# Two layers of a hybrid decoder trunk on one core: groups of two picks, adds ahead of some rows, and a reordered opening

## The reference

```
h = rms_norm(x);  proj = h @ w_in          # q, k, v, forget logits, pool part, state-space part
x = x + concat(norm(attention), norm(pool), norm(s5)) @ w_out
h = rms_norm(x)                            # PEER
q = h @ w_q;  scores against 2 x 128 sub-keys per head (8 heads)
top 16 of each half -> 256 candidates -> top 16 -> expert index = i1*128 + i2, gates = softmax
u_sel, v_sel = u_tab[experts], v_tab[experts]       # 128 picks per token, rows of 1024 floats
x = x + sum_k gate_k * gelu(h . u_sel_k) * v_sel_k
```

## Time and profile before

| what | value |
|---|---|
| median of three runs | 1546.36 us |
| profiled execution, its own time | 1547.98 us |
| its span from first to last instruction | 1546.1 us |
| granted TensorE clock, mean over the span | 0.826 |
| busy in the span | DVE 70%, PE 68%, POOL 40%, ACT 37% |
| moved in the span | 623.55 MB, 403 GB/s on average |
| q0 (gathers) | 536.90 MB, 83.7% of the 16 engines' span |
| q1 (SP's transfers) | 85.41 MB, 13.4% |

### The profile page before, as it was taken

How to read it: one execution, slowest core, us unless ns; L and a number is a source line. 1 busy time by engine, 2 the same in 40 slices (tenths; PEclk the granted TensorE clock), 3 DMA queues, 4 the chain that set the end, 5 groups by cost and what they waited for, 6 DMA issues and landing times. The chain is left out here.

```text
span 1546.1 us, 19439 instructions
## 1 busy us (share of the span) xinstructions
PE 1049.1 (68%) x6790; PEld 532.8 (34%) x6790; DVE 1083.2 (70%) x2485; ACT 575.1 (37%) x1768; POOL 619.7 (40%) x571
## 2 busy tenths in 40 slices
PE   8898656785854668776775667788588465565555
PEld 6685312333531334332552334333255111111111
DVE  8777998646999685654789767564579965444444
ACT  5544433623444433441544431354234432221222
POOL 0034345442753533443343433444243354455441
PEclk9999877887986988787897788889698777667767
DMA  9289999999999999999999999999999999999997
GB/s 381 89 326 421 420 421 420 421 421 405 422 421 368 411 422 421 421 421 421 409 421 421 421 421 421 421 422 420 422 386 421 421 421 422 421 421 422 421 421 304
DMA packets 86642, 623.55 MB, mean 403 GB/s; under 512 B 10000, under 2 KB 10128, under 8 KB 11792
## 3 DMA queue, kind: packets, MB, share of 16 engines
q0 software_dynamic: 73728, 536.90, 83.7%
q1 hardware_dynamic: 12816, 85.41, 13.4%
HBM read 621.23 MB, written 1.05 MB: 402 GB/s over the span
## 5 line engine op out<-in xcount | busy, mean ns | idle before, releaser
L583 POOL DMA_INDIRECT slots<-experts,idx x512 | 593.2, 1159 | 886.5 <-PE psum L1830 709.9
L1427 DVE CUSTOM_DVE_ANT_0 slots<-slots,h 128x1024 f32<-128x1024 f32 x512 | 615.9, 1225 | 390.8 <-DMA slots<-experts,idx 387.6
L1830 PE MATMUL psum<-slots,diag 64*64 64x512 f32 x4088 | 599.3, 737 | 312.4 <-ACT diag L947 312.3
L1830 PEld LDWEIGHTS psum<-slots,diag 64*64 64x64 f32 x4088 | 175.8, 165 | 684.2 <-ACT diag L947 368.9
L931 ACT ACTIVATE ge<-ge 128x4 f32<-128x4 f32 x130 | 26.7, 205 | 437.3 <-DVE ge L1427 436.3
L1752 PE MATMUL psum<-hT,ring 128*128 128x128 f32 x992 | 131.3, 297 | 20.7 <-DMA ring<-weights 16.0
L931 ACT ACT_TABLE_LOAD x55 | 70.6, 1283 | 194.7 <-DVE ge L1427 194.3
L947 ACT ACTIVATE diag<-cst,ge 128x64 f32<-128x64 f32 x511 | 136.5, 336 | 6.7 <-PE psum L1830 2.5
L1752 PEld LDWEIGHTS psum<-hT,ring 128*128 128x128 f32 x992 | 127.7, 212 | 23.5 <-issue 17.7
L938 ACT ACTIVATE ge<-ge,gate 128x1 f32<-128x1 f32 x512 | 109.1, 283 | 4.2
L1525 PE MATMUL psum<-ring,hT 128*128 128x256 f32 x192 | 52.2, 433 | 17.5 <-DVE work L981 17.5
(11 more groups left out here) (292 smaller groups left out, 1075.4 us busy)
## 6 DMA issues: line engine op xcount, KB each, us to landing
ring<-weights SPq DMA_DIRECT2D x32, 1152.0 KB, 10.0
ring<-weights SPq DMA_DIRECT2D x26, 1024.0 KB, 9.2
slots<-weights SPq DMA_DIRECT2D x11, 1024.0 KB, 20.0
slots<-experts,idx POOLq DMA_INDIRECT x512, 20.8
ring<-weights SPq DMA_DIRECT2D x2, 1056.0 KB
sml<-small SPq DMA_DIRECT2D x2, 652.0 KB, 9.1
slots<-weights SPq DMA_DIRECT2D x1, 1056.0 KB, 9.0
xs<-x SPq DMA_DIRECT2D x2, 512.0 KB, 13.2
```

Source lines behind the costliest of these rows:

```text
L583: pool.indirect_dma_start(out=slot[:, place(E), :], out_offset=None, in_=src, in_offset=bass.IndirectOffsetOnAxis(ap=idx[:, n % 2, e:e + 1 ...
L1427: ins = dve.tensor_tensor_reduce(u, u, h2[:, n % 2, :], 1.0, 0.0, ALU.mult, ALU.add, d[:, i:i + 1])
L1830: ins = pe.matmul(acc[HALF * half:HALF * half + HALF, i, :], diag[rows, d % DIAGS, :], slot[rows, place(E), D + half * 512:D + half * 512 ...
```

## The change

There are four edits.

1. `GRP` is 2 in place of 4: 64 groups a step. A group is weighed and added by itself, and a row now stands at the next border of two picks. The last two picks remain groups of one.
2. A new piece `adds` on PE: ahead of a row that contains one of the twelve names in `FOLLOWS`, PE adds the group that is waiting, which otherwise it would do behind the row.
3. `MIX0` is in another order. `mul1` and `mul2` come behind `cm`, `mul3` behind `mixp`. `qkn0` (the sums of squares) comes ahead of `scan0`, and the subtraction of `scan0` becomes a piece of its own (`scan_im`) behind `qkn1`. At the end of `MIX0`, `p`, `qkv0` and `qkv1` of step 1 come ahead of the routing of head 1.
4. SP loads the first q block right behind the chunk of the pool part.

```
-GRP = 4
+GRP = 2
...
-        "power4", "qkv0", "f", "prep", "fx", "ln", "mul0", "mul1", "mul2", "mul3", "rotate0", "rotate1", "cum", "cm",
-        "qkv1", "rotate2", "bu", "qkv2", "scan0", "qkv3", "qkn0", "scan1", "qkn1", "qkv4", "pool", "qkT", "pre0", "pre1",
-        "mixp", "sq1", "scan2", "scan3", "scan4", "scan5", "scan6", "logits0", "scan7", "big0", "logits1", "scan8",
...
+        "power4", "qkv0", "f", "prep", "fx", "ln", "mul0", "rotate0", "rotate1", "cum", "cm", "mul1", "mul2",
+        "qkv1", "rotate2", "bu", "qkv2", "qkv3", "qkn0", "scan0", "qkn1", "scan_im", "qkv4", "pool", "qkT", "pre0", "pre1",
+        "mixp", "mul3", "sq1", "scan1", "scan2", "scan3", "scan4", "scan5", "scan6", "logits0", "scan7", "big0", "logits1",
...
+        "route0", ("xT", 1), ("hTe", 1), "rp1", ("u", 1), "soft0", ("uT", 1), ("p", 1), ("up", 1), ("qkv0", 1),
+        ("f", 1), ("fx", 1), ("ln", 1), ("qkv1", 1), "route1", "soft1", ("cum", 1), ("cm", 1), ("qkv2", 1), ("qkv3", 1),
...
+FOLLOWS = {"normT", "u", "qkv0", "y", "glu", "qkT", "att1", "att2", "att3", "att4", "out0", "h2T"}
...
                 step, row = rows[at]
+                if FOLLOWS.intersection(row):
+                    order.append(("mix", "adds", n))
                 order += [("mix", s, 2 if s[:3] == "tab" else step) for s in row]
...
             chunk(CH_SSM)
             chunk(CH_POOL)
+            chunk(CH_Q)
             sp.dma_start(cst[:, P:], consts[:, P:]).then_inc(S["cst_in"], 16)
             drive_(0)
             rest_(0)
-            for i in range(6):
+            for i in range(1, 6):
                 chunk(CH_Q + i)
...
+            def scan_im(n):
+                link(tt(w3[1], w3[1], w3[3], ALU.subtract))
...
                 if part % 9 == 0:
                     link(tt(w3[0], w3[0], spare, ALU.add))
-                    link(tt(w3[1], w3[1], w3[3], ALU.subtract))
+                if part == 9:
+                    scan_im(n)
...
+            def adds(n):
+                add_last()
```

More of the change, by code:

```diff
@@ L136, in script @@
                 order += [("mix", "soft" + s[5:], step) for s in row if s[:5] == "route"]
-    for quad in (QUADS, QUADS + 1):
-        order += [("open", n, quad), ("close", n, quad)]
-    return order + [("mix", "drain", STEPS - 1)]
+    return order + [("open", n, QUADS), ("close", n, QUADS), ("mix", "drain", STEPS - 1)]
 ORDER = script()
@@ L191, in experts_of @@
     start, end = PICKS * n + GRP * quad, PICKS * n + GRP * quad + GRP
[L192 to L195, removed]
+    last = PICKS * STEPS - 1
+    return range(start, min(end, last)) if start <= last else range(last, last + 1)
 BY_VECTOR = {PICKS * STEPS - 1}
@@ L203, in by_tensor @@
     return sum(1 for e in range(E) if e not in BY_VECTOR)
-G_LAST = QUADS * STEPS + 1
+G_LAST = QUADS * STEPS
 SECTION = (slice(0, 512), slice(512, 768), slice(768, 1024))
@@ L1428, in dots @@
                 told(ins, "dots_ready")
-            run(dict(inverse=inverse, fold=fold, attg=attg, x1p=x1p, x1a=x1a, h2=h2_, power=power, rotate=rotate_, normA=normA, normT=normT, uT=u_out, cum=cum,
+            run(dict(scan_im=scan_im, inverse=inverse, fold=fold, attg=attg, x1p=x1p, x1a=x1a, h2=h2_, power=power, rotate=rotate_, normA=normA, normT=normT, uT=u_out, cum=cum,
                      warm=blank, h2T=h2T, turnback=turnback, bu=bu, scan=scan, backA=back, backB=back_im, y=y_, glu=glu, qkn=qkn, qkT=qkT,
@@ L1838, in close @@
                 waiting.append((n, quad))
-            run(dict(warm=warm, pre=pre, logits=logits0, turn=turn0, pv=pv0, normT=normT, xT=normT, u=u, p=p_, f=f_, oua=out_a, bu=bu, qkv=qkv, y=y_, glu=glu, qkT=qkT, att=att, pool=pool_,
+            run(dict(adds=adds, warm=warm, pre=pre, logits=logits0, turn=turn0, pv=pv0, normT=normT, xT=normT, u=u, p=p_, f=f_, oua=out_a, bu=bu, qkv=qkv, y=y_, glu=glu, qkT=qkT, att=att, pool=pool_,
                      mixp=mixp, merge=merge, out=out_b, h2T=h2T, rp=rp, route=route), lambda n, quad: None, close)
```

## The result

The changed kernel takes 1551.45 us (median of 8 runs, 1548.9 to 1552.9) against 1546.5 (8 runs): ratio 1.0028, 95% interval 1.0019 to 1.0037. It is 4.3 us slower by the ratio, where 9.4 us faster was forecast. The profiled execution took 1550.07 us, its span is 1548.3.

What follows compares the result with a forecast made beforehand. Transfers at 421 GB/s bound most of the span, DVE's routing the 450 us stretch; 1.9 + 5.8 + 1.7 = 9.4 us off 1547.98 gives 1538.6, as a median 1537.0. Range 1534.5 to 1540; over all cases 1532.5 to 1544.5.

Steps and rivals of the forecast that it cites:

- The opening: Start up to the first gather: first maximum and all after it 1.9 us earlier.
- the four times shown above: Opening: sum of squares at 35.27 us, scaling from about 38.1, first maximum 46.1, first gather near 84.3.
- 0.2 us in hand for the squares: Opening: ACT's squares ready near 35.1 us, just in time for DVE's sum at 35.27.
- The row h2T: Near 370, 750 and 1120 us: slots freed earlier keep transfers full, 5.8 us won over three steps.
- length x (1 - rate/421): The prediction's measure of time in which transfers stand, per window; the short ones add up to 11.5 us.
- The end of step 0: 450 to 515 us: DVE waits 0.8 us per routing row; transfers stand 4.0 instead of 5.7 us, 1.7 won.
- It holds: Up to about 250 us: six routing rows cost 4.8 us, covered by 4.2 in hand and pairs freed 3.2 earlier.
- the end of step 2: Said to have six such routing rows too; a hole near 1240 us would make the forecast wrong.
- PE's adds cost nothing where transfers are full: Other stretches: PE's adds, like the doubled number of gelus, were priced at nothing.
- The slower rival: Routing rows where DVE is the bound: wait spreads, 2.1 us a row, 1552.7 us; decides from 1.2; chance 0.07.
- the wait behind the pair: Routing rows: DVE waits for ACT's score copy behind a pair's weighing, 0.8 us taken, 2.1 in the slower rival.

Runs made afterwards that it cites:

- e2: The kernel before with only the adds ahead of the twelve kinds of rows, in groups of four with the old opening: ratio 1.0005.
- e5: The kernel before, in groups of four, with the new opening and adds ahead of the row h2T only: ratio 0.9993.
- e7: The changed kernel with no adds ahead of rows, and ACT copying a head's scores before weighing the pair ahead of its row: ratio 0.9995.
- e8: As e7, with routing rows spaced out (each counts 1.5 rows when rows are spread over pairs): ratio 0.9999 to the kernel before.
- e10: e8 with the gather of pick 500 held back until an add seven later than its slot needs: ratio 0.9995 to the kernel before.
- e4: The changed kernel without the adds ahead of att1 to att4 and out0: ratio 0.9992 to the kernel before.
- e9: The changed kernel measured again, unedited: ratio 1.0035 to the kernel before.
- e1: The kernel before with the new opening alone, in groups of four, nothing added ahead of rows: ratio 0.9991.
- e3: The kernel before in pairs only, with the old opening and nothing added ahead of rows: ratio 1.0005.
- e11: e8 with the gather of pick 500 held back by nine adds: ratio 1.0027 to the kernel before.
- e12: e8 with the gather of pick 500 held back by eleven adds: ratio 1.0055 to the kernel before.

## Why the prediction was wrong

**The opening: right in the trace, sized too well.** Each of the four times shown above fell within 0.05 us of the forecast. But it hung on 0.2 us in hand for the squares, which seven of eleven executions did not have, and on PE keeping its clock near 52 us, which four did not: 0.8 us on average where 1.9 was taken.

**The row h2T: the first step that failed.** "All of 1.5 + 1.1 + 3.2 = 5.8 us comes back": the mean rate did, the time did not. e2 and e5 show the gain of step 2 returned as a hole at 1240, for DVE bounds the stretch from 1157 to 1250, and transfers that are ahead find full slots. And the sum itself was wrong: length x (1 - rate/421) counts engines that run dry early, where the slowest of them ran on and set the end. Of the 11.5 us only 2.25 were at a share of one engine or none, and 0.64 had no packet under way. e7, e8 and e10 show this by the time.

**The end of step 0: right as a hole, nothing as time.** 3.4 us where 4.0 were forecast (its own terms add up to 4.1 to 4.2: the last sum is 36.3, and two waits of 0.8 are 1.6), 0.65 us of wait where 0.8 was. e7 takes the wait away and e8 spaces out the rows; neither wins what can be told from no change. "It holds" was right for the stretch up to 250 us, where five rows waited 0.75 us each and the transfers stayed full. For the end of step 2, which the prediction put beside it, it was wrong by 5.5 us of missing rate; e4, with 4.8 missing there and a time no worse than that of before, shows that this cost nothing that can be told.

**The cost that was not seen: the second step that failed.** "PE's adds cost nothing where transfers are full" put the adds ahead of rows at nothing, without a reason. The prediction followed what adds ahead of a row free, and never asked what then stands behind them: in att1 to att4 it is the logits, that is DVE, ACT's exp and the very diagonals that the next adds wait for. e4 prices it at 5.6 us, more than the whole loss. With the opening's 0.8 to 1.4 gained and the rest at zero, about the 4.3 measured follow.

Why the ring costs as much as 5.6 us is only in part shown. Its hole has 6.6 us missing, but no engine at work for just 1.43 of them, 0.92 in e9; e2 has the ring with 4.1 missing and never fewer than two engines at work, and loses nothing that can be told. That all engines stand fits every kernel that is slower than the one before, but the remaining 4 us of the changed kernel are open: the engine that still works in a hole need not be the one that is last at the end, and the trace doesn't say which engine a packet is of.

The slower rival had the sign and not the cause: the wait behind the pair was 0.65 us, below the 1.2 from which it was to decide. Its hole at the end of step 2 did open, and cost nothing that can be told.

No kernel here beats the one before by more than the measurement can tell; e1 and e4, at 0.9991 and 0.9992, come nearest. D is 1450.6 to 1452.7 in all but the four whose engines all stood for over a microsecond. Still open, besides the rest of the ring's price: which DMA engine is last and why, and why the holes of one and the same order differ between executions (e8 misses 1.9 us at 445 to 520, e10, equal up to pick 500, 6.2). "Alone" ranks the kernels at its two ends only: e3 has 3.25 and loses nothing. "None" separates the slower ones from the others, but does not give the size of their loss.

## What to carry to other kernels

When work is moved ahead of a step, write down what now stands behind it and follow it round: if the moved work waits for an engine that waits for that step, a ring closes, and its period against the time of the transfers says whether they can run dry (13.70 us against 9.96 here). What that costs has to be measured: it was 5.6 us with pairs and the new opening, and nothing that can be told in e2. Read a hole in a transfer-bound kernel by its lowest share, not by its area: while the engine that is last still works, the area is backlog being evened out. In e10, 3.8 us of it were free, and in e11 and e12 the time beyond was not. Where an engine is the bound over a whole stretch, a hole closed at its start opens at its end.

## What was not expected of the hardware

The 16 DMA engines can be 8 us apart at the end of 1450 us of transfers (share 0.07 from 1528 to 1536 in e8), in kernels whose mean rate shows a full 421 GB/s. A gather could be issued 19.6 us later and its data be used only 0.1 us later. And a short wait of PE can cost more than itself: behind the 3.61 us of the ring 32 matmuls take 6.29 us, in the kernel before 3.67 at the full clock and 6.03 behind a wait of 2.66 us and eight matmuls; behind 2.25 us in the opening the clock fell in all four executions that had this wait, and the first gather came as late as with the old opening in some of them (86.15 and 86.35).
